# A fused GLA and ConvFFN layer on one core: weight sums of the up-projection kept in DRAM, and the work at the feed-forward block edges reordered

## The reference, cut to what matters

```python
x = x + mixer(rmsnorm(x, norm1), ...)        # short convolution and gated linear attention
x = x + conv_ffn(rmsnorm(x, norm2), ...)
y = rmsnorm(x, final_norm)

def conv_ffn(xn, prev, w_up, conv_w, w_down):
    u = xn @ w_up                            # 1024 x 5632
    uc, new = causal_dwconv(u, prev, conv_w) # 3 taps over positions
    a, g = jnp.split(uc, 2, axis=-1)         # D_FF = 2816 each
    return (jax.nn.silu(g) * a) @ w_down, new
```

## Time and profile before

| | before |
|---|---|
| runs | 2570.39, 2574.65, 2572.38 us |
| the profiled execution | 2569.17 us, of which the span in the trace is 2567.4 us |
| PE busy | 2361.4 us (92%) |
| DVE busy | 1817.1 us (71%) |
| POOL busy | 1499.1 us (58%) |
| ACT busy | 1072.5 us (42%) |
| DRAM traffic | 197.32 MB read, 32.83 MB written |

### The profile page before, as it was taken

One profiled execution on the slowest core, in us unless ns is written; L12 is line 12 of the kernel. 1 busy time (PEld: TensorE's weight loads), 2 busy tenths in 40 slices (PEclk: granted clock), 3 DMA queues, 4 the chain that ended last, 5 costly groups with the idle time before them and its releaser, 6 DMA issues. The chain is left out here.

```text
span 2567.4 us, 39164 instructions
## 1 busy us (share of the span) xinstructions
PE 2361.4 (92%) x13090; PEld 2144.5 (84%) x13090; DVE 1817.1 (71%) x2588; ACT 1072.5 (42%) x2059; POOL 1499.1 (58%) x1487
## 2 busy tenths in 40 slices
PE   7999969999969996999999997999999978889896
PEld 6899858899768985899999986999999967778785
DVE  2045650255631666788988997889988978999998
ACT  4233353333343334444444445444444454444443
POOL 4132413222332344887777786887778777777773
PEclk9999989999979998999999998999999989999998
DMA  5121351112252235322222244122222333222222
GB/s 155 50 58 42 123 201 58 50 42 90 101 179 65 67 107 206 116 64 74 74 74 65 63 154 148 55 68 74 74 74 61 118 124 94 74 74 74 74 76 69
DMA packets 244718, 231.43 MB, mean 90 GB/s; under 512 B 8060, under 2 KB 216273, under 8 KB 244625
## 3 DMA queue, kind: packets, MB, share of 16 engines
q1 hardware_dynamic: 244625, 230.18, 28.4%
HBM read 197.32 MB, written 32.83 MB: 90 GB/s over the span
## 5 line engine op out<-in xcount | busy, mean ns | idle before, releaser
L1233 PE MATMUL ps<-xo,wq_hi 128*128 128x384 f32 (+1 forms) x1848 | 606.8, 328 | 92.4 <-DVE r L1891 41.3
L436 POOL TENSOR_TENSOR w_lo<-raw,w_hi 128x512 fp32r<-128x512 f32 x192 | 252.3, 1338 | 605.9 <-ACT w_hi L429 605.9
L1234 PE MATMUL ps<-xo,wq_lo 128*128 128x384 f32 (+1 forms) x1848 | 602.7, 326 | 0.0
L1235 PE MATMUL ps<-xo,wq_hi 128*128 128x384 f32 (+1 forms) x1848 | 602.3, 326 | 0.0
L763 POOL TENSOR_TENSOR wq_lo<-wu_sum,wq_hi 128x256 fp32r<-128x256 f32 x528 | 465.5, 907 | 208.9 <-ACT wq_hi L858 203.6
L1811 DVE TENSOR_TENSOR resid<-resid,ps 128x512 f32<-128x512 f32 (+1 forms) x748 | 487.1, 678 | 13.2 <-PE ps L1235 4.4
L1233 PEld LDWEIGHTS ps<-xo,wq_hi 128*128 128x128 f32 x1848 | 354.5, 192 | 128.4 <-issue 74.6
L763 POOL TENSOR_TENSOR wq_lo<-wu_raw,wq_hi 128x256 fp32r<-128x256 f32 x396 | 401.3, 1033 | 28.0 <-ACT wq_hi L858 28.0
L1828 DVE SCALAR_TENSOR_TENSOR up_y<-up_u,params,up_y 128x768 f32<-128x768 f32 (+1 forms) x264 | 342.9, 1299 | 52.1 <-ACT up_y L888 27.5
L1234 PEld LDWEIGHTS ps<-xo,wq_lo 128*128 128x128 f32 x1848 | 354.9, 192 | 18.7
L1235 PEld LDWEIGHTS ps<-xo,wq_hi 128*128 128x128 f32 x1848 | 354.9, 192 | 0.0
(11 more groups left out here) (191 smaller groups left out, 3817.5 us busy)
## 6 DMA issues: line engine op xcount, KB each, us to landing
wu_raw<-in_w_up_dram SPq DMA_DIRECT2D x132, 512.0 KB, 5.0
raw<-in_w_in_dram SPq DMA_DIRECT2D x72, 512.0 KB, 3.9
wd_raw<-in_w_down_dram SPq DMA_DIRECT2D x66, 512.0 KB, 5.7
x_in<-in_x_prompt_dram SPq DMA_DIRECT2D x32, 512.0 KB, 4.8
raw<-in_w_out_dram SPq DMA_DIRECT2D x24, 512.0 KB, 3.4
xo_raw<-x_ops SPq DMA_DIRECT2D x14, 768.0 KB, 5.5
x_mid<-resid SPq DMA_DIRECT2D x16, 512.0 KB, 2.6
resid<-x_mid SPq DMA_DIRECT2D x16, 512.0 KB, 6.4
```

What stands on the lines that cost most here:

```text
L436: last = pool.tensor_tensor(w_lo[:, s, r], raw[:, s, r], w_hi[:, s, r].bitcast(F32), ALU.subtract)
L1233: pe.matmul(out, lh, rh, start=(first and n == 0), stop=False, skip_group_check=skip)
L1234: pe.matmul(out, ll, rh, start=False, stop=False, skip_group_check=skip)
L1235: last = pe.matmul(out, lh, rl, start=False, stop=end, skip_group_check=skip)
```

## The change

- A DRAM tensor `w_sums` of 22 x 1 MB is added. In the first block DVE makes the sums as before, and SP stores each step's four sums there (`store_sums`). In the two other blocks DVE makes none: SP loads them into `wu_sum` (`load_sums`), after `low_up(g, 6)` has released it, and `high_up(g+1, 1)` on ACT waits for the load instead of DVE.
- In the last step of a block the load of the next block's first sums stands in SP's queue behind the seven operand loads.
- `low_x(b, 6)` goes from POOL to DVE. In the first block operands 4, 5 and 6 are split inside step 0 instead of ahead of it.
- The final norm of tiles 4 and 5 goes from the end of step 1 to its middle, with one pair of table loads fewer. The stores and loads of rows 0 and 1 go behind the loads of `wu_raw` in step 0.
- In the last step of all, no down-projection of step 20 is made inside step 21; all ten stand behind it.

The diff, cut to its core:

```diff
 def head_shares(b, f):
+    if b == NB - 1 and isinstance(f, int) and f == NF - 2:
+        return shares([0] * NP, 0)
 def tail_shares(b, f):
+    if b == NB - 1 and isinstance(f, int) and f == NF - 2:
+        return shares([2 * TILES[b]], 0)
...
+        w_sums = nc.dram_tensor("w_sums", [NF, P, 4, 512], F32).ap()
...
-        LOW_BY_V = (0, 1, 3, 5)
-        LOW_BY_P = (2, 4, 6)
+        LOW_BY_V = (0, 1, 3, 5, 6)
+        LOW_BY_P = (2, 4)
...
+            def store_sums(f):
+                sp.dma_start(w_sums[bass.ds(f, 1)].rearrange("o p n c -> p (o n) c"), wu_sum[:, :, :]).then_inc(wu_stored, 16)
+
+            def load_sums(f):
+                sp.dma_start(wu_sum[:, :, :], w_sums[bass.ds(f, 1)].rearrange("o p n c -> p (o n) c")).then_inc(wu_cached, 16)
...
             sp.wait_ge(wu_summed, 4)
+            store_sums(0)
             sp.wait_ge(wu_lo, 6)
             load_up(0, 1)
...
+                last_f = is_last(f)
+                if last_f and b + 1 < NB:
                     for i in range(NP):
                         sp.wait_ge(up_done, NP * g + i + 1)
                         load_x_op(b + 1, i)
+                if b < NB - 1 or not last_f:
+                    if b or last_f:
+                        sp.wait_ge(wu_lo, NP * (g + 1))
+                        sp.wait_ge(wu_stored, 16 * NF)
+                        load_sums(0 if last_f else f + 1)
+                    else:
+                        sp.wait_ge(wu_summed, 4 * (g + 2))
+                        store_sums(f + 1)
+                if isinstance(f, int) and f == 1 and b:
+                    results(b, range(2, TILES[b - 1]))
                 if more:
-                    sp.wait_ge(wu_summed, 4 * (g + 2))
                     sp.wait_ge(wu_lo, NP * (g + 1) + 6)
                     load_up(b, f + 2 if not isinstance(f, int) or f + 2 < NF else f + 2 - NF)
+                if isinstance(f, int) and f == 0 and b:
+                    results(b, range(2))
...
+            def sums_ready(g, n, cached):
+                if cached:
+                    act.wait_ge(wu_cached, 16 * (g - NF + 1))
+                else:
+                    act.wait_ge(wu_summed, 4 * g + n + 1)
...
-            for i in range(3, NP):
-                if i == 4:
-                    mixes[NB - 1].wait(act, "out_done", 8 * TILES[NB - 1])
-                if i < NP - 1:
-                    if i in A_SUM:
-                        act.wait_ge(wu_summed, A_SUM[i] + 1)
-                    high_up(0, i)
-                high_x(0, i)
+            act.wait_ge(wu_summed, S3 + 1)
+            high_up(0, 3)
+            high_x(0, 3)
+            mixes[NB - 1].wait(act, "out_done", 8 * TILES[NB - 1])
+            high_up(0, 4)
+            high_up(0, 5)
...
-                    act.wait_ge(wu_summed, 4 * (g + 1) + S2 + 1)
+                    sums_ready(g + 1, S2, b > 0 or is_last(f))
                     high_up(g + 1, 1)
...
-                if edge == 0 and b:
+                if edge == 0:
                     high_x(b, 6)
+                if edge == 1 and b:
+                    for t in range(4, TILES[b - 1]):
+                        final_rstd(b - 1, t)
+                    act.preload_act_table(ACT.Silu)
...
@@ DVE, ffn_step
-                if more:
+                if b == 0 and not is_last(f):
                     sum_up(g + 1, 0)
                     sum_up(g + 1, 1)
...
                 adds(4)
+                if edge == 0:
+                    low_x(b, 6)
+                if edge == 1 and b:
+                    for t in range(4, TILES[b - 1]):
+                        final_scale(b - 1, t)
```

More of the change, by code:

```diff
@@ L347, in build @@
         wu_loaded, wu_summed, wu_hi, wu_lo = sem("wu_loaded"), sem("wu_summed"), sem("wu_hi"), sem("wu_lo")
+        wu_stored, wu_cached = sem("wu_stored"), sem("wu_cached")
         wd_loaded, wd_high, wd_low = sem("wd_loaded"), sem("wd_high"), sem("wd_low")
@@ L657, in ffn_step, with results @@
                         load_x_op(b + 1, i)
+                if b < NB - 1 or not last_f:
[8 more added lines that the diff above has]
+                    results(b, range(2, TILES[b - 1]))
                 if more:
-                    sp.wait_ge(wu_summed, 4 * (g + 2))
                     sp.wait_ge(wu_lo, NP * (g + 1) + 6)
                     load_up(b, f + 2 if not isinstance(f, int) or f + 2 < NF else f + 2 - NF)
+                if isinstance(f, int) and f == 0 and b:
+                    results(b, range(2))
+            def results(b, tiles):
+                for t in tiles:
+                    store_result(b - 1, t)
+                    if t < TILES[b]:
+                        load_resid(b, t)
             for b in range(NB):
@@ L800, in _ @@
             low_up(0, 4)
-            low_x(0, 4)
             low_up(0, 5)
-            low_x(0, 6)
             def ffn_step(b, f, par, more=True):
                 g = b * NF + f
-                first_f = isinstance(f, int) and f == 0 and b > 0
+                first_f = isinstance(f, int) and f == 0
                 prev = before(b, f, 1)
@@ L1164, in ffn_step @@
                     final_rstd(b - 1, 3)
-                    act.preload_act_table(ACT.Silu)
                 if more:
@@ L1204, in ffn_step @@
                     high_x(b + 1, 3)
-                if edge in (0, 1) and b:
+                if edge == 0 and b:
                     act.preload_act_table_set("natural_log_exp_and_others")
-                    for t in range(2) if edge == 0 else range(4, TILES[b - 1]):
+                    for t in range(2):
                         final_rstd(b - 1, t)
@@ L1535, in _ @@
             b = NB - 1
+            down_ready(b, NF - 2)
             for share in tail_shares(b, NF - 2):
@@ L1580, in sum_up @@
                     wait(dve, wu_lo, NP * g)
+                    wait(dve, wu_stored, 16 * g)
                     dve.tensor_tensor(s1, g0, g1, ALU.add).then_inc(wu_summed, 1)
@@ L1908, in ffn_step @@
                 add_taps(b, 1, f, y_g, taps_g)
-                if edge == 1 and b:
-                    for t in range(4, TILES[b - 1]):
-                        final_scale(b - 1, t)
                 dve.wait_ge(up_done, NP * g + 7)
```

13 lines of the change are left out of this document (2 added, 11 removed).

## The result

The changed kernel takes 2609.7 us (median of 4 runs, 2607.9 to 2611.2). The kernel before took 2571.8 us beside it. The ratio is 1.0144, interval 1.0132 to 1.0157: slower by 37.9 us. I had predicted 2569, with a range of 2540 to 2600.

What follows compares the result with a forecast made beforehand. PE bounds the first two blocks, DVE (through `r_3`) the third. Third block -4, edges -5, start +6, end -0.5 give -3.5 on the profiled 2569.2, so 2565.7; the median, 3.2 higher, is predicted as 2569, range 2540 to 2600.

Steps and rivals of the forecast that it cites:

- I take 20.8 us: Third block's step, from a loop of landing 9.7, ACT 0.7 and POOL 10.9 less savings; 21.0 before, -4 us in all.
- I take 0.2 off: Third block, POOL's 10.9 us: 0.3 off for sums leaving DVE, 0.2 more for DVE's taps coming beside other POOL work.
- my ceiling, 21.8: Third block's longest forecast step: POOL as now and the landing 0.5 later, +15 us in all.
- The fit of the Trainium skill that the prediction names: Transfer cost of about 2.0 us fixed plus bytes at 436 GB/s; 1 MB behind a backlog adds 2.4, where 2.6 was taken.
- Followed through the queues,: Block edges: 15 us late on ACT, 14 late mid step 0, 3 at its last product, 2.5 early in step 2; -2.5 per edge.
- the edge stall is not made good: Rival at the two edges: less than 14 of the 15 us come back, +7 an edge, 2593 us in all; chance 0.24.
- DVE ... is busy without a break: End of the kernel: DVE has the same work up to the last norm wherever the down-projections stand; -0.5 us.
- my split of it into 2.6 and 3.8: Start of the feed-forward: 2.6 for the first sums' store, 3.8 for operand 6's rounding, split and `c21`; +6 after shrinking waits.
- My ceiling there: Middle block: loop at most 1.8 longer than the third's, 22.6 under PE's 22.8; at the ceilings +0.3 x 20 = +6.
- free POOL: Rival: without the sums on DVE POOL runs free, third block 20.0 us a step, edges catch up, 2543 us; chance 0.20.
- PE's pace: Rival in the third block: the load is hidden and a step takes 17.5 us, 2507 us in all; chance 0.04.
- the added traffic: Rival: traffic reaches the middle block too (+6), third block 21.8 (+15), edges +3 each, start +6; 2605 us; chance 0.08.

Runs made afterwards that it cites:

- e3: The changed kernel with the `wd_raw` load behind the sums load in SP's queue in blocks two and three, same bytes; 2586.5 us.
- e1: The changed kernel with DVE making the weight sums again in the third block from step 1 on; 2596.9 us.
- e2: The changed kernel with the load of the next block's first sums ahead of the seven operand loads at both edges; 2578.0 us.
- e6: The changed kernel with no sums stored or loaded, DVE making all of them, the reordering kept; 2558.7 us.
- e10: e6 with the low part of operand 6 back on POOL behind `low_down`; 2572.9 us.
- e11: e6 with the norms of tiles 4 and 5 back at the end of step 1 and SP's result stores back ahead of the weight loads; 2564.7 us.
- e12: e9 with the last step's shares as before and operands 4 to 6 of the first block split ahead of step 0 as before; 2532.4 us.
- e8: The changed kernel with the store of the first sums behind the first two `wu_raw` loads of step 1; 2611.6 us.
- e4: The changed kernel with the sums load cut in two: S1 to S3 go out after `low_up 4`, S4 after `low_up 6`, same bytes; 2554.2 us.
- e5: The changed kernel with the last two steps' down-projections shared out as before, four of them inside the last step; 2611.0 us.
- e9: The changed kernel with sums and `wu_raw` loads cut and issued where buffers come free, g0 left out, first sums ahead of operands at the edges; 2540.5 us.

## Why the prediction was wrong

**The third block's loop: right mechanism, term mis-sized.** "I take 20.8 us" was 22.1 in the trace. In the turn shown the landing was 10.2 for 9.7, and POOL's stretch 11.1 for 10.4; over the 17 steps the means are 10.1 and 11.4. So most of the miss, 1.0 us of 1.3, is POOL's. The failing step is "I take 0.2 off" with the 0.3 before it: the sums left DVE, but POOL's stretch got no shorter than the 10.9 of the earlier trace rows. `low_up 1` did shrink, from 1.73 to 1.44. But from the end of `low_up 2` to the start of `low_up 5` POOL took 6.3 (2353.5 to 2359.79), before 5.8 (2220.28 to 2226.06). The half microsecond is in `low_up 3` and `low_up 4`, 3.36 instead of 2.84, and it is there in every one of the 17 steps. In the kernel before DVE's first taps started behind these two; POOL, then DVE:

```profile
2220.24 2.84 POOL L763 TENSOR_TENSOR wq_lo<-wu_sum,wq_hi 128x256 fp32r<-128x256 f32 x4
2223.03 3.07 POOL L788 TENSOR_TENSOR wd_lo<-wd_raw,wd_hi 128x512 fp32r<-128x512 f32 x2
...
2223.40 1.54 DVE L1828 SCALAR_TENSOR_TENSOR up_y<-up_u,params,up_y 128x578 f32<-128x578 f32 x1 [0.52 <-ACT up_y L888]
```

In the changed kernel they start while the two still run:

```profile
2354.85 1.39 DVE L1862 SCALAR_TENSOR_TENSOR up_y<-up_u,params,up_y 128x578 f32<-128x578 f32 x1 [5.11 <-ACT up_y L919]
```

The Trainium skill ("SBUF — State Buffer", "Who interferes with whom") says that a DVE instruction with two inputs in SBUF contends with a GpSimd instruction that reads SBUF. That agrees with both: the sums went from beside `low_up 1`, and the taps came beside `low_up 4`, so the rule gave no gain here. Even my ceiling, 21.8, was below. The 17 steps of the row lost 19.1 us where I had given -4: 23 us off. The landing was 0.4 late on the mean, against a price taken at another place of the program; why is not shown. e3 shows that the backlog is real (1.26 us for the 512 KB). The fit of the Trainium skill that the prediction names stands there for transfers that GpSimd issues, and these are SP's; it entered no sum.

**The last step: left out.** I counted the loop for steps 2 to 20 and took the last step as it was, 17.4. But the stretch from 2547.71 to 2570.73 still holds one wait for a load, that of the sums of step 21: ACT stood 4.1 us for it, and DVE 5.3 for ACT's `y_g` behind it. The stretch took 23.0. e1, without the loop, has 17.7. 5.6 us.

**The edges: the stall right, the recovery wrong.** The stall came as computed. I then let 15 us of it be made good in the steps behind, "Followed through the queues,". e2 shows the stall at its full price, 16.0 and 11.5, and e2 against before shows the recovery's true size, 13.2 and 7.7. What I called recovery was a gain of its own that existed without the stall (e6: 10.0 and 7.2); the two add, they do not overlap. Its parts in e10 and e11 are 3.5 and 3.6 for operand 6, 6.0 and 2.8 for the norms with the stores. 12 us over both edges. The edges took 2.9 and 3.8 more than before, between my -2.5 and the +7 of the rival "the edge stall is not made good".

**The end: wrong in sign.** "DVE ... is busy without a break" was not true of the place that the adds left: there they filled DVE's waits for ACT's taps. Without them DVE waits, and further on the adds wait for their matmuls. +3.4 instead of -0.5.

**Right:** the start (+6.0), though my split of it into 2.6 and 3.8 is not shown. Without the store 3.4 stay (e6); with the store but the splits as before 4.3 stay at step 2 (e12, 1086.01 against 1081.68); the store's place in the queue gives nothing (e8). Each of the two alone leaves more than half of it, so they do not add up as I had it, and the exact hit is partly luck. The middle block (22.81) is right too, but by less than I thought: it is at the limit, as e1 and e2 show. My ceiling there was also worked out wrong, since 21.8 + 1.8 is 0.8 above 22.8 and not 0.3. No free POOL, no PE's pace. The rival that came nearest in time, the added traffic (2605), is refuted by e4, and its time came about by other terms.

Together: 23 + 5.6 + 12 + 4 = 44 on the profiled execution, rounded. Its forecast was 2565.7, and it took 2609.7 (1.8 more than its span).

## What to carry to other kernels

When work on an idle-enough engine is replaced by a load into a single buffer, draw the circle from the buffer's last reader through the queue to its first reader, and put each piece's load behind that piece's own last reader: here keeping the sums in DRAM cost 51 us in one order of the loads (2609.7 - 2558.7). With every load moved to where its buffer comes free it was 18 faster than without the sums in DRAM (2558.7 - 2540.5); that comparison also holds the earlier `wu_raw` loads and the bytes left out, which no run tests apart. A load that is needed first must not stand in a queue behind loads that wait for late events. A stall and a gain at the same place add up, as they did at both edges here, unless a trace shows idle time that both would use. And work that leaves an engine moves the work behind it: look at what it will then run beside.

## What the runs showed of the hardware

Twice the same DVE instruction, the split of operand 5 (two inputs in SBUF), at the first edge: first in the changed kernel, then in e5.

```profile
1562.68 2.03 DVE L1605 TENSOR_TENSOR xo<-xo_raw,xo 128x1536 fp32r<-128x1536 f32 x1 [0.62 <-ACT xo L895]
```

```profile
1561.23 9.21 DVE L1600 TENSOR_TENSOR xo<-xo_raw,xo 128x1536 fp32r<-128x1536 f32 x1 [0.90 <-ACT xo L891]
```

In e5 it began at 1561.23, while POOL ran short instructions without a gap up to 1568.83, ten of them from 1560.83 on, and it ended at 1570.44, 1.6 us behind them. PE stood still for 7.3 us. In the thirteen other traces no split of an operand took over 2.8. All four runs of e5 took 2608.2 to 2613.8, so the event may well be in each of them; only one has a trace. It is not confined to splits: taps of 2.9 to 5.9 us stand in e9 (16), e12 (15) and e11 (2), where the kernel before has none over 2.7, and every one in e9 and e12 ends 0.6 us behind a stretch that POOL ran without a gap. So the two engines do not only slow each other by tenths: DVE can be held for a whole run of POOL's instructions. A run without a gap does not suffice, as the 2.03 of the changed kernel shows, beside which POOL ran without one too; what decides which engine gives way no run shows. Here is POOL beside the split of e5:

```profile
1560.83 1.45 POOL L787 TENSOR_TENSOR wq_lo<-wu_sum,wq_hi 128x256 fp32r<-128x256 f32 x2
1562.23 1.43 POOL L787 TENSOR_TENSOR wq_lo<-wu_raw,wq_hi 128x256 fp32r<-128x256 f32 x2
1563.61 2.78 POOL L787 TENSOR_TENSOR wq_lo<-wu_sum,wq_hi 128x256 fp32r<-128x256 f32 x4
1566.34 2.49 POOL L812 TENSOR_TENSOR wd_lo<-wd_raw,wd_hi 128x512 fp32r<-128x512 f32 x2
```
